# VectorE takes GpSimd's weight splits, and the second mixer's gates and long convolution run between the steps of its attention heads

## The reference, cut to what matters

```python
def swiglu(h, w1, w3, w2):
    return (jax.nn.silu(h @ w1) * (h @ w3)) @ w2

for l in range(2):                                    # first_block
    m = (cond @ w_mod[l] + b_mod[l]).reshape(bsz, 3, 3, D_MODEL)
    x = x + 0.5 * m[:, 0, 2] * swiglu(adaln_in(x, norm_g[l, 0], m, 0), ffn_w1[l, 0], ...)
    h = adaln_in(x, norm_g[l, 1], m, 1) @ w_in[l]     # 640 columns of q, k, v, then 3 x 512
    mix = mixer_ab(h, ...) if l % 2 == 0 else mixer_cd(h, ...)
    x = x + m[:, 1, 2] * (mix @ w_out[l])
    x = x + 0.5 * m[:, 2, 2] * swiglu(adaln_in(x, norm_g[l, 2], m, 2), ffn_w1[l, 1], ...)

def mixer_cd(h, ...):
    q, k, v = split_qkv(h, qk_g)
    att = blocked_dense_attention(axial_rope(q), axial_rope(k), v)   # 8 heads of 64
    u = short_conv(h[..., QKV_COLS:], conv_w, conv_b)                # 3 taps
    x0, x1, vh = jnp.split(u, 3, axis=-1)
    z = x1 * vh
    y = x0 * (fft_long_conv(z, kfull) + skip * z)
    return jnp.concatenate([att, y], axis=-1)
```

## Time and profile before

| | us |
|---|---|
| median of 3 runs | 1671.08 |
| lowest and highest | 1668.28, 1674.58 |
| the profiled execution | 1669.29 |
| its span | 1667.5 |
| mean granted TensorE clock in it | 0.942 |

### The profile page before, as it was taken

The page is one execution under the profiler, slowest core; times in us unless marked ns, Lnnn a source line. Parts: engine busy times, 40 slices in busy tenths (PEclk is TensorE's granted clock), DMA queues, the critical chain, the costliest instruction groups (busy, mean ns, idle before and its releaser), DMA issues.

```text
span 1667.5 us, 26869 instructions
## 1 busy us (share of the span) xinstructions
PE 1502.6 (90%) x10982; PEld 1386.0 (83%) x10982; DVE 1231.4 (74%) x1766; ACT 687.6 (41%) x1085; POOL 527.2 (32%) x248
## 2 busy tenths in 40 slices
PE   1999988899999999999896999999986689789998
PEld 1999988688999989999793789999853478589998
DVE  6899987657888879897647575654746556489998
ACT  2343444344333433334432444434345445444443
POOL 0232334241233322243345113323443223023333
PEclk8999999999999999999897999999997799799999
DMA  9977772145777546765430235555201113135552
GB/s 392 383 302 294 278 296 95 49 185 228 305 295 288 216 200 274 286 239 197 154 146 26 93 136 223 194 190 200 99 3 63 63 57 130 71 123 190 190 190 76
DMA packets 32329, 309.29 MB, mean 185 GB/s; under 512 B 3496, under 2 KB 5800, under 8 KB 7504
## 3 DMA queue, kind: packets, MB, share of 16 engines
q1 hardware_dynamic: 32208, 307.59, 48.2%
HBM read 306.51 MB, written 1.06 MB: 184 GB/s over the span
## 4 chain that ended last, share of the span: by engine, by line
PE 76%; DVE 15%; issue 3%; ACT 3%; DMA 2%; POOL 1%; SPq 0%; DVEq 0%; ACTq 0%; POOLq 0%
PE bank L735 13%; PE bank L604 11%; PE bank L600 11%; PE bank L601 10%; PE bank L658 5%; PE bank L653 5%; PE bank L655 5%; PE bank L570 2%; DVE WL L1468 2%; PE bank L617 2%; PE bank L799 2%; DVE scr L1524 2%; PE bank L810 1%; DVE scr L1559 1%; PE bank L765 1%
## 5 line engine op out<-in xcount | busy, mean ns | idle before, releaser
L1411 POOL TENSOR_TENSOR WL<-ring,WH 128x1024 fp32r<-128x1024 f32 x168 | 459.2, 2738 | 1041.5 <-ACT WH L1004 1041.5
L1004 ACT ACTIVATE WH<-ring 128x1024 fp32r<-128x1024 f32 x420 | 429.5, 1053 | 150.6 <-PE bank L735 67.2
L1468 DVE TENSOR_TENSOR WL<-ring,WH 128x1024 fp32r<-128x1024 f32 x252 | 372.3, 1480 | 94.4 <-ACT WH L1004 94.3
L600 PE MATMUL bank<-XH,WH 128*128 128x256 f32 x1680 | 409.7, 283 | 1.6 <-ACT WH L1004 1.6
L601 PE MATMUL bank<-XL,WH 128*128 128x256 f32 x1680 | 406.8, 281 | 0.0
L600 PEld LDWEIGHTS bank<-XH,WH 128*128 128x128 f32 x1680 | 316.4, 188 | 8.0 <-issue 4.9
L601 PEld LDWEIGHTS bank<-XL,WH 128*128 128x128 f32 x1680 | 316.4, 188 | 1.0 <-issue 1.0
L604 PE MATMUL bank<-XH,WL 128*128 128x256 f32 x1680 | 233.4, 281 | 5.2 <-DVE WL L1468 5.2
L604 PEld LDWEIGHTS bank<-XH,WL 128*128 128x128 f32 x1680 | 213.3, 188 | 6.2 <-DVE WL L1468 6.2
L653 PE MATMUL bank<-GH,WH 128*128 128x256 f32 x840 | 202.6, 280 | 1.7 <-DVE GL L1592 1.7
L655 PE MATMUL bank<-GL,WH 128*128 128x256 f32 x840 | 202.4, 280 | 0.0
(11 more groups left out here) (263 smaller groups left out, 1957.3 us busy)
## 6 DMA issues: line engine op xcount, KB each, us to landing
ring<-in_stream SPq DMA_DIRECT2D x132, 1536.0 KB, 6.6
scr<-in_stream SPq DMA_DIRECT2D x15, 1536.0 KB, 10.8
PR<-in_stream SPq DMA_DIRECT2D x15, 1536.0 KB, 8.3
att<-in_stream SPq DMA_DIRECT2D x15, 1536.0 KB, 10.1
ring<-in_stream SPq DMA_DIRECT2D x9, 1024.0 KB, 5.1
ring<-in_stream SPq DMA_DIRECT2D x11, 512.0 KB, 3.6
kf_mix<-in_stream SPq DMA_DIRECT2D x2, 1536.0 KB, 16.1
con<-in_consts SPq DMA_DIRECT2D x1, 2112.0 KB, 13.0
```

The source lines that it names most:

```text
L600: pe.matmul(o, part(WH, u, k), XH[:, k, :], start=(k == 0), stop=False)
L1004: act.activation(part_all(WH, u), raw(u), ACT.Copy).then_inc(*mark("high", u))
L1411: pool.tensor_tensor(part_all(WL, u), raw(u), part_all(WH, u).bitcast(F32), ALU.subtract)\
L1468: dve.tensor_tensor(part_all(WL, u), raw(u), part_all(WH, u).bitcast(F32), ALU.subtract)\
```

## The change

1. `low_engine`: the low splits of w2 in blocks 0 to 3, and all of `win0`, `wout0`, `win1` and `wout1`, are VectorE's. GpSimd makes none before `win2`.
2. End of a block: in the last chunk VectorE makes no splits; the first unit of the next stage is split low after the eight additions. The fills of PR's borders move a chunk earlier. TensorE makes all eight outputs and then the eight sums of the norm. In two norms VectorE makes the low splits of the next block's first units between scaling and low parts; at the start ScalarE too splits them before the high parts.
3. `win0`: TensorE takes unit 10 ahead of head 0 (`lead`), units 11 to 18 inside the heads. VectorE works `conv_unit(10 + h)` and the low split of unit 14 + h inside head h.
4. `win1`: its columns are reordered (second and third part by pairs, gate last). Units 0 to 13 come first, with the rotation after unit 9; unit 14 is the `lead`, 15 to 18 are worked in heads 0, 1, 3 and 5. The convolution reads PSUM: ScalarE takes the middle tap and the bias, VectorE two taps. The transposes of z are in head 1, the spectra in heads 2 and 4, their products in 3 and 5, the inverse in 6 and 7, the gating in 7 and after. ScalarE prepares skip * z in head 3. The attention's halves go to `MH`, `ML`, its banks are 3 and 6, the convolution's 2 and 7.
5. In attention "m" the norm sum of head 7 moves behind its transposes.

```diff
@@ low_engine
-    if name[0] == "win0" and name[1] >= 7:
-        return "pool"
-    if name[0] in ("w1", "w3", "w2"):
-        return "pool" if name[0] == "w2" else "dve"
-    if name[0] in ("win0", "win1") and name[1] >= 12:
-        return "pool"
-    if name[0] in ("wout0", "wout1") and name[1] < 3:
-        return "pool"
+    if name[0] == "w2":
+        return "pool" if name[1] == 4 else "dve"
+    if name[0] in ("w1", "w3", "win0", "wout0", "win1", "wout1"):
+        return "dve"
     return "pool" if name[1] % 2 else "dve"
@@ tensor, ffn, down(c) for the last chunk
                             last.then_inc(*mark("ffn_out", f, m))
-                            if follows and m >= 4:
-                                if m == 4:
-                                    take(6, "stat_root", follows)
-                                norm_sum_chunk(follows, m - 4)
                         if follows:
-                            norm_end(follows, 4)
+                            take(6, "stat_root", follows)
+                            norm_end(follows, 0)
@@ tensor, win0_and_attention
                 def fill(h, k):
-                    last = passes(10 + h, [("hh", "hl", "lh")[k]])
+                    last = passes(11 + h, [("hh", "hl", "lh")[k]])
...
-                attention("a", lambda h: [("head_normed", "a", 5)], fill=fill)
-                unit("win0", passes, 18)
+                attention("a", lambda h: [("head_normed", "a", 5)], fill=fill, lead=lambda: unit("win0", passes, 10))
@@ tensor, win1_and_attention
+                for j in range(2, 8):
+                    unit("win1", passes, j)
+                head_sum("c")
+                unit("win1", passes, 8)
+                head_spread("c")
+                unit("win1", passes, 9)
+                rope("c")
+                for j in range(10, 14):
+                    unit("win1", passes, j)
+                def fill(h, k):
+                    units = {0: 15, 1: 16, 3: 17, 5: 18}
+                    if h in units:
+                        last = passes(units[h], [("hh", "hl", "lh")[k]])
...
+                    if h == 1 and k == 1:
+                        z_transposes()
+                    if h in (2, 4) and k == 2:
+                        z_spectrum(h // 2 - 1)
+                    if h >= 6 and k < 2:
+                        convolve(2 * (h - 6) + k)
@@ scalar
-            def norm(k, waits):
+            def norm(k, waits, ahead=-1):
                 load_table(ACT.Sqrt)
                 squares(k, waits)
                 root(k)
+                split_to(ahead)
                 highs(k)
+            def middle_tap(j):
+                i = WIN1_ORDER[j] - 7
+                act.wait_ge(*at("product", "win1", j))
+                act.activation(short_dst(j), src_of("win1", j), ACT.Identity, bias=prm("dconv_b", i),
+                               scale=prm("dconv_w", 12 + i)).then_inc(*mark("middle_tap", j))
+            def win1_with_head(h):
+                units = {0: 14, 1: 15, 2: 16, 4: 17, 6: 18}
+                if h == 2:
+                    for t in range(2):
+                        act.wait_ge(*at("z_turned", t))
+                        act.activation(ZT[:, t, :], bank[CONV_BANK[t]], ACT.Copy).then_inc(*mark("z_copied", t))
+                if h in units:
+                    middle_tap(units[h])
+                    split_to(first_unit("win1") + units[h] + PARTS)
...
             def win0_with_head(h):
-                j = 9 + h
+                j = 10 + h
                 if conv_role(j)[1] == "input":
                     win0_copy(j)
                 split_to(first_unit("win0") + j + PARTS)
@@ gpsimd
-                if name == ("win1", 18):
...
-                    for c in range(4):
-                        pool_conv(MIX[:, 4 + c, :], VH[:, 0, :], PR[:, 7 + c, :], PADL - 1, 3,
-                                  lambda k: prm("dconv_w", 12 * k + c), prm("dconv_b", c), ("gate_conv", c))
@@ vector, ffn
-                    split_to(up_units(f, c)[1] + PARTS)
+                    ends = f < 4 and c == NFF - 1
+                    if not ends:
+                        split_to(up_units(f, c)[1] + PARTS)
                     mod_rows(f, c, 0)
...
-                    if c > 0:
+                    if c > 0 and not ends:
                         split_to(UNIT_AT["w2", f, c - 1] + PARTS)
...
+                split_to(UNIT_AT["w2", f, NFF - 1] + 1)
@@ vector, win0
+                    split_to(u0 + 7 + PARTS)
                     head_inverse("a")
                     head_scale("a")
...
+                    split_to(u0 + 8 + PARTS)
                     conv_unit(8)
+                    conv_unit(9)
+                    split_to(u0 + 9 + PARTS)
                     dve.wait_ge(*at("rel_in"))
-                    attention("a", lambda h: conv_unit(9 + h))
-                    conv_unit(17)
+                    def with_head(h):
+                        conv_unit(10 + h)
+                        split_to(u0 + 10 + h + PARTS)
+                    attention("a", with_head)
                     conv_unit(18)
@@ vector, win1
                     def short_conv(j):
...
+                        dve.wait_ge(*at("middle_tap", j))
+                        link(dve.scalar_tensor_tensor(o[:, 1:S], src[:, 0:S - 1], prm("dconv_w", i), o[:, 1:S], ALU.mult, ALU.add))
+                        dve.scalar_tensor_tensor(o[:, 0:S - 1], src[:, 1:S], prm("dconv_w", 24 + i), o[:, 0:S - 1],
+                                                 ALU.mult, ALU.add).then_inc(*mark("short_conv", j))
+                    split_to(u0 + 10)
+                    short_conv(7)
+                    head_inverse("c")
+                    split_to(u0 + 11)
+                    short_conv(8)
+                    z_mul(0)
+                    head_scale("c")
+                    split_to(u0 + 12)
+                    short_conv(9)
+                    rope("c", 0, 3)
+                    split_to(u0 + 13)
+                    short_conv(10)
+                    z_mul(1)
+                    rope("c", 3, 3)
+                    for j in range(11, 14):
+                        split_to(u0 + j + 3)
+                        short_conv(j)
+                    z_mul(2)
+                    split_to(u0 + 17)
+                    def with_head(h):
+                        units = {0: 14, 1: 15, 2: 16, 4: 17, 6: 18}
+                        if h in units:
+                            short_conv(units[h])
+                            split_to(u0 + units[h] + PARTS)
+                        if h == 0:
+                            z_mul(3)
+                        if h in (3, 5):
+                            spectra_mult((h - 3) // 2)
+                        if h == 7:
+                            gated(0)
+                            gated(1)
+                    attention("c", with_head)
+                    gated(2)
+                    gated(3)
```

More of the change, by code:

```diff
@@ L138 @@
 WIN0_ORDER = list(range(7)) + [k + c for c in range(4) for k in (11, 15, 7)]
+WIN1_ORDER = list(range(7)) + [k + c for c in range(4) for k in (11, 15)] + list(range(7, 11))
 def conv_role(j):
@@ L230, in halves @@
     def halves(name):
-        return (MH, ML) if name in ("a", "wout0") else (XH, XL)
+        return (MH, ML) if name in ("a", "wout0", "c", "wout1") else (XH, XL)
     mod_slots = [scr[:, 0:ITEM], scr[:, ITEM:2 * ITEM], pr_flat[:, 0:ITEM], att[:, :], kf_mix[:, 0:ITEM],
@@ L415, in proj_bank @@
     def proj_bank(name, j):
-        return j % 2 if name == "win0" and j >= 8 else j % 4
+        return j % 2 if name == "win0" and j >= 8 or name == "win1" and j >= 13 else j % 4
     RESID = ("wout0", "wout1", "wout2", "wmo")
@@ new lines, in convolve, with win1_and_attention @@
+            def convolve(c):
+                pe.wait_ge(*at("spectra_mult", 1))
+                take(CONV_BANK[c], "convolved", c)
+                for i in range(4):
+                    a2, f = i // 2, i % 2
+                    last = pe.matmul(bank[CONV_BANK[c]][:, 0:S], Y[:, a2, f, c * P:(c + 1) * P],
+                                     cst("ci" if a2 == 0 else "si", f * S, S), start=(i == 0), stop=(i == 3))
+                last.then_inc(*mark("conv_sum", c))
+            def win1_and_attention():
+                passes = projection("win1", *norm_parts(("sub", 1, 1)))
+                proj_first("win1", passes)
+                for j in range(2, 8):
[11 more added lines that the diff above has]
+                        last = passes(units[h], [("hh", "hl", "lh")[k]])
+                        if k == 2:
+                            last.then_inc(*mark("product", "win1", units[h]))
+                    if h == 1 and k == 1:
[4 more added lines that the diff above has]
+                        convolve(2 * (h - 6) + k)
+                attention("c", lambda h: [("rotated", "c", h // 2), ("rotated", "c", 4 + h // 4)], fill=fill,
+                          lead=lambda: unit("win1", passes, 14))
```

225 lines of the change are left out of this document (105 added, 120 removed).

## The result

The changed kernel takes 1645.4 us at the median (1643.5 to 1647.0, four runs), the kernel before 1672.8 in the runs beside it (1668.3 to 1674.6): ratio 0.984, 95% interval 0.982 to 0.986. That is 27 us, where 18 had been forecast against the median.

What follows compares the result with a forecast made beforehand. TensorE, busy 90% of the span, was taken as the bound, so only its pauses and lower clock pay. Terms -4.3 - 3.0 - 14.6 + 9.2 - 3.9 - 0.5 = -17.1 us, giving 1653, range 1635 to 1668.

Steps and rivals of the forecast that it cites:

- Blocks: Feed-forward blocks: w2 low splits moved to VectorE end four TensorE waits, -5.3, one comes in, +1.0; sum -4.3 us.
- rival B: First block: VectorE overflows, busy 201.5 us, 17 over the block; kernel at 1677 us; chance 0.05.
- The late low split of its second w1 unit: Third block: this low split now comes after the first gated product, later than TensorE wants it: +1.0 us.
- Block ends: Four block ends: 13.47, 9.24, 11.58 and 9.86 us become 7.4 each, together -14.6 us.
- Rival D: Block ends give half because something unseen is late next; kernel at 1661 us; chance 0.17.
- Start: First up-product: weight units split ahead of the norm's parts, its last third starts near 46.5 instead of 49.84: -3.0 us.
- First mixer: Front +1.4 and -1.6, attention +9.4 from VectorE waiting for ScalarE's high split behind the pair copy: +9.2 us.
- Rival A: Attention heads: the waits bite less, +9.4 becomes about -2, second mixer gains 6 more; kernel at 1636 us; chance 0.2.
- Second mixer: Stretches of 61.6 and 38.2 us become 33.4 and 58.1, -8.3; with clock and late split, sum -3.9 us.
- the lower clock after head 6: Second mixer: TensorE at its lower clock after head 6 costs +3 us.
- Rival C: Both attentions: TensorE stays at its lower clock, +25 us, +34 at worst; kernel at 1678 us; chance 0.08.
- Elsewhere: Third attention: one norm sum moves behind the transposes, -0.5 us.

Runs made afterwards that it cites:

- experiment 2: Kernel before with one part each: w2 low splits of blocks 0 to 3 on VectorE, 1662.0 us (0.994); new block ends only, 1661.2 us (0.994).
- experiment 1: Changed kernel with the w2 low splits of the first four blocks back on GpSimd: 1652.6 us, ratio 0.990 to the kernel before.
- experiment 7: Changed kernel with VectorE one head later in both attentions, plus the last block's w2 low splits on VectorE: 1626.6 us, ratio 0.972.
- experiment 4: Changed kernel, first attention: VectorE's low split one head later, 1628.8 us (0.975); or ScalarE's high split before its pair copy, 1630.9 us (0.977).
- experiment 5: Changed kernel with ScalarE's middle tap and high split before the pair copy in the second attention: 1638.5 us, ratio 0.982.

## Why the prediction was right, and where its sizes were off

**Blocks: the mechanism right, the term too small.** No VectorE low split is slow while GpSimd rests, block 0 is at 156.8 us of VectorE work (159 counted), and experiment 2 gives block 0 its exact length from the engine choice alone. The rule of the Trainium skill (SBUF — State Buffer, Who interferes with whom) is borne out on both sides: operations between SBUF operands take 2.62 or up to 3.4 us beside a GpSimd instruction and 0.42 or 1.22 without, while the product with a PSUM operand is at 0.42 in both. The cast is delayed too (0.56 instead of 0.29 in the mean), though it has one SBUF input: the prediction left out that the page makes an exception of VectorE's 2-port modes. Which mode this cast runs in no run shows. The other page (Perfetto Trace Analysis, Optimizing Scalar/DVE Operations) would relieve a saturated VectorE by other engines; experiment 1 measured the opposite for GpSimd in the time, experiment 7 in VectorE's busy time alone, and rival B, built on it, fell.

The step that was too small is the sum of the waits, and nothing was counted for the clock. Block 0 gave 3.5 us where its two waits had been put at 2.85. Block 2 gave 2.6 where 1.4 had been counted. With the engine choice alone (experiment 2, first kernel) it gave 2.85; with the new ends alone it became 1.3 us longer. The late low split of its second w1 unit did come, and TensorE stands idle 0.96 us for it until 593.82; most of that is made up by a lower clock that ends sooner. Block 1 changed by 0.1 and block 3 gave 1.0, where nothing had been counted and where no matmul waited before. The first 10 us after the norm of block 2, before and after:

```profile
588.24:598.24 10.00, 9.99 (x50) 9.07 (x51) 5.25 (x14) 3.97 (x9) 0.00 (x0) 0.66 0.32 138
```

```profile
581.81:591.81 10.00, 10.00 (x57) 9.28 (x58) 6.77 (x16) 4.74 (x10) 0.00 (x0) 0.71 0.43 157
```

That is 57 matmuls instead of 50. The pause of TensorE for the norm (3.5 us) is the same. The granted clock falls to 0.5 once around it, before the change 0.6 us after the first matmul that follows, after the change 1.1 us ahead of it, so that it is back 5.7 instead of 7.4 us after that matmul. In block 3 it is back after 5.6 instead of 7.9 us; 2.3 us less at half speed are 1.2, and block 3 gave 1.0. This is not a gain of the new block ends: before block 3 stands `wout1` and no block end, the kernel with the new ends alone has 8.2 there and the one with the engine choice alone 5.0, and kernels with the changed kernel's code for block 3 have anything from 5.6 to 7.2. What places the fall stays open; some 2 of the 6.9 us hang on it and are luck.

**Block ends: right.** 7.4 each was said and 7.66 measured, the same at all four; the last quarter of a microsecond stays open. Experiment 2 shows the order to be the cause. Rival D fell.

**Start: right**, 1 us larger than counted, and within its bounds.

**First mixer: the total right, with luck, two of its terms wrong.** The heads came as worked out: 7.6, 6.2, 10.1, 7.3, 10.2, 7.3, 7.5 against 6.6, 6.3, 10.2, 6.6, 10.2, 6.3, 8.8, together 56.2 against 55.0. The wait in front (+1.4, the second unit's low split behind the norm's low parts) is not to be seen: TensorE has no gap from 239.9 to 287.7. In its place stands a stretch at the lower clock before head 0 that was not forecast:

```profile
276.90:290.15 13.25, 10.77 (x59) 9.33 (x58) 10.63 (x25) 3.36 (x10) 0.00 (x0) 0.74 0.00 0
```

The 24 matmuls of one unit follow each other there at 0.213 us instead of 0.118, 2.2 us in all, though TensorE had not paused before them. From the norm to head 0 TensorE is busy 5.4 us longer (2.8 for unit 10, most of the rest the lower clock) and idle 3.5 us less (2.1 at head 0, and a pause of 1.4 us that went). That is +1.9, the number forecast, by another sum. The seven heads came out 1.2 us over the sum worked out for them with the lower clock in it, where 3 had been put on top for that clock. And the clock moves the total: four profiled kernels with the same code in this mixer took 141.6, 143.7, 147.1 and 147.6 us, which is +6.2 to +12.3 where +9.2 was forecast. Rival A, that the waits would not bite, fell: they bit as told. What they cost in all was set too low: the prediction had the heads without them 11.4 us shorter (rival A), and experiment 4 found 17.2 in that stretch. The kernel came out 8 us under the forecast for other reasons.

**Second mixer: the balance right, the additions wrong.** The two stretches of the earlier trace rows are 34.6 and 58.3 us now, against 33.4 and 58.1 worked out. The heads were 5.9, 6.6, 8.4, 5.8, 7.4, 5.8, 9.0. What failed is the step "the lower clock after head 6: +3; the late low split in front: +1.4". The front grew by 0.7 us, without a gap in TensorE's work, and the lower clock did not come. It is 0.97 from head 0 to `wout1`, where it had been 0.78 before; the heads had been worked out without a lower clock and 3 us were put on top for it, but from the first to the last transposes it stayed at 1.00, though TensorE was idle for 8.3 us there. Rival C fell with it in this kernel, though experiment 5 shows how near it is for the first attention (0.76 in one execution), and what makes the one attention lose its clock and the other not stays open.

**Elsewhere: within its own spread.** -2.5 instead of -0.5, in pieces of about 1 us. Kernels with the same code after block 3 took 493.8 to 498.1 us there, so this is nothing to explain by the change.

## What to carry to other kernels

Take work between SBUF operands off GpSimd when VectorE runs beside it, even if VectorE looks full: its busy time holds the other's instructions, so price the move at the undisturbed durations. But an instruction placed on an engine in program order brings its wait along: before it is put ahead of something urgent, ask when what it waits for is made, and what that stands behind; one step later in the order was worth 17 us of its stretch here and 14 to 17 of the time, more than half of what the whole change gave. When a pause is removed, look for the clock too: more than a third of those 17 us was TensorE at its lower clock after the pauses.

## What the runs showed of the hardware that was not expected

- The delay beside GpSimd also falls on VectorE's cast (0.294 to 0.559 us in the mean) and on its multiply-and-sum rows (1.28 to 1.87). In a loop with a steady beat it can fall on the same instruction every time: 2.62 us in each of twelve chunks of the last block.
- The same attention code ran at granted clocks of 0.94, 0.88, 0.80 and 0.76 in four profiles, in 54.9, 56.2, 60.2 and 61.6 us. Pauses of up to 4.3 us in some of the heads leave TensorE partly at 1.2 GHz, by an amount that differs from run to run; with the pauses gone the clock was 1.00. The second attention kept 1.00 with 8.3 us of pauses in 49.1.
- The clock can fall without a pause: it fell to 0.5 at 276.9, when TensorE had been busy without a gap for 37 us, the last of them with the head norm's small matmuls (0.216 us apart), and the 24 matmuls of one unit ran at the lower clock.
